# One gate chain for both directions of the mLSTM, the backward rows in reversed time

## The reference

```
gates = (g[0], log_sigmoid(g[1]), g[2], log_sigmoid(g[3]))   # input, forget; forward, backward
b = cumsum(fc);  m_t = max(b + m, running max of (b_t - b_s + i_s));  m_new = m_t of the last step
h_b, st_b = mlstm_scan(_flip(q), _flip(k), _flip(v), _flip(logi_b), _flip(logf_b), init_b, ...)
h = h_f + _flip(h_b)
```

## Time and profile before

| | |
|---|---|
| median of three runs | 2566.61 us |
| the profiled execution's own time | 2568.26 us |
| its span | 2566.5 us |
| TensorE busy, mean granted clock | 2237.9 us (87%), 0.922 |
| VectorE, ScalarE busy | 1160.2 us (45%), 887.2 us (35%) |
| HBM read | 672.15 MB, 262 GB/s over the span |
| x mixers (by the trace) | from about 1812 and 2186 us |

### The profile page before, as it was taken

The page is one execution under the profiler, slowest core; times in us unless marked ns, Lnnn a source line. Parts: engine busy times, 40 slices in busy tenths (PEclk is TensorE's granted clock), DMA queues, the critical chain, the costliest instruction groups (busy, mean ns, idle before and its releaser), DMA issues. The chain is left out here.

```text
span 2566.5 us, 45132 instructions
## 1 busy us (share of the span) xinstructions
PE 2237.9 (87%) x19490; PEld 1800.9 (70%) x19490; DVE 1160.2 (45%) x2084; ACT 887.2 (35%) x1478; POOL 58.3 (2%) x78
## 2 busy tenths in 40 slices
PE   6998788887786899879999999787897999888998
PEld 6967465554553887766766766464777998767997
DVE  5355345323331653543333322532677554766554
ACT  4444232233210542332222211232544443534442
POOL 0000000000000000000000000000000000000000
PEclk9999888989897999989999999888888999988999
DMA  7594998999999656758999999977632555323551
GB/s 237 161 337 161 365 347 337 355 377 391 405 373 363 229 185 225 283 190 327 393 395 393 390 384 376 349 284 297 206 99 84 185 177 171 132 68 115 181 173 41
DMA packets 254367, 676.24 MB, mean 263 GB/s; under 512 B 12624, under 2 KB 65872, under 8 KB 254160
## 3 DMA queue, kind: packets, MB, share of 16 engines
q1 hardware_dynamic: 238832, 614.75, 64.7%
q0 software_dynamic: 15328, 58.50, 6.7%
HBM read 672.15 MB, written 1.05 MB: 262 GB/s over the span
## 5 line engine op out<-in xcount | busy, mean ns | idle before, releaser
L444 PE MATMUL bank<-xx,high 128*128 128x256 f32 (+1 forms) x3296 | 640.9, 296 | 41.1 <-DVE xx L583 26.3
L444 PEld LDWEIGHTS bank<-xx,high 128*128 128x128 f32 (+1 forms) x3296 | 530.6, 197 | 100.1 <-issue 71.5
L444 PE MATMUL bank<-xx,low 128*128 128x256 f32 (+1 forms) x1648 | 479.1, 291 | 0.0
L444 PEld LDWEIGHTS bank<-xx,low 128*128 128x128 f32 (+1 forms) x1648 | 325.3, 197 | 1.6
L393 DVE TENSOR_TENSOR low<-lane,high 128x1024 fp32r<-128x1024 f32 (+1 forms) x112 | 130.7, 1170 | 366.8 <-ACT high L382 366.8
L382 ACT ACTIVATE high<-lane 128x1024 fp32r<-128x1024 f32 (+1 forms) x112 | 113.0, 1012 | 336.1 <-PE bank L444 336.1
L444 PE MATMUL bank<-hx,high 128*128 128x256 f32 x1056 | 201.3, 292 | 0.0
L444 PEld LDWEIGHTS bank<-hx,high 128*128 128x128 f32 x1056 | 167.4, 194 | 18.1 <-issue 16.3
L444 PE MATMUL bank<-hx,low 128*128 128x256 f32 x528 | 150.9, 286 | 0.0
L1335 ACT ACTIVATE hs<-bank 64x256 f32<-64x256 f32 x64 | 24.2, 377 | 317.6 <-PE bank L1322 317.5
L1342 DVE TENSOR_TENSOR hs<-hs,bank 64x256 f32<-64x256 f32 x64 | 27.1, 423 | 224.4 <-ACT hs L1335 224.4
(11 more groups left out here) (539 smaller groups left out, 4126.7 us busy)
## 6 DMA issues: line engine op xcount, KB each, us to landing
ring__13<-in_expert_w_gu SPq DMA_DIRECT2D x52, 1024.0 KB, 11.1
ring__12<-in_expert_w_gu SPq DMA_DIRECT2D x51, 1024.0 KB, 11.2
ring__14<-in_expert_w_gu SPq DMA_DIRECT2D x51, 1024.0 KB, 11.4
ring__56<-in_expert_w_gu SPq DMA_DIRECT2D x26, 1024.0 KB, 10.7
ring__12<-in_expert_w_down SPq DMA_DIRECT2D x26, 1024.0 KB, 9.8
ring__154<-in_expert_w_gu SPq DMA_DIRECT2D x26, 1024.0 KB, 12.7
ring__55<-in_expert_w_gu SPq DMA_DIRECT2D x25, 1024.0 KB, 10.8
ring__14<-in_expert_w_down SPq DMA_DIRECT2D x25, 1024.0 KB, 9.7
```

The lines of the kernel that those rows point to most:

```text
L444: done = pe.matmul(out, a.bitcast(F32R), b.bitcast(F32R), start=it["start"] and k == 0 and q == 0 and not halves, stop=stop)
```

## The change

The 16 gate rows are put on 8 partitions of two buffers: rows 0 to 3 forward, rows 4 to 7 backward, the backward ones in reversed time. A new table of zeros and ones, `gsel`, and a second matmul that reads `graw` from right to left do that. One chain then serves both directions over steps s = 0, 1 (for the backward direction chunk 1 - a); it has 19 operations and 20 turns. The copy to nw and the difference that follows it now share a turn. Behind `in_done` ScalarE writes m_t and U once more from right to left (the two lines added in `act`), and the gate columns of d = 1 come from those; `decay_pe` reads nw from right to left for d = 1. In `ln_at` the 32 becomes 20. Besides, ones_r and zeros shrink from 128 columns to one, which is broadcast where it is read. The diff, without its unchanged lines:

```diff
@@ -45,7 +45,7 @@
-          ("eps", 1), ("jota", NX), ("flip", 1), ("odd", 1), ("pick", 16)):
+          ("eps", 1), ("jota", NX), ("flip", 1), ("odd", 1), ("pick", 16), ("gsel", 32)):
@@ -158,11 +158,11 @@
-row, ones_r, pick = space(ctx, "row", NROW), space(ctx, "ones_r", P), space(ctx, "pick", 16)
+row, ones_r, pick = space(ctx, "row", NROW), space(ctx, "ones_r", 1), space(ctx, "pick", 16)
...
-zeros = space(ctx, "zeros", P)
+zeros = space(ctx, "zeros", 1)
@@ -174,7 +174,7 @@
-    return row[q:q + 2, o + a:o + (wd if n is None else a + n)].bitcast(F32R), ones_r[q:q + 2, :].bitcast(F32R)
+    return row[q:q + 2, o + a:o + (wd if n is None else a + n)].bitcast(F32R), ones_r[q:q + 2, :].bitcast(F32R).to_broadcast([2, P])
@@ -415,7 +415,7 @@
-                pe.matmul(z, zeros[:, 0:z.shape[0]].bitcast(F32R), some.bitcast(F32R), start=True, stop=False)
+                pe.matmul(z, zeros.bitcast(F32R).to_broadcast([P, z.shape[0]]), some.bitcast(F32R), start=True, stop=False)
@@ -817,9 +817,9 @@
-        act.activation(ones_r.bitcast(F32R), ones, ACT.Copy)
+        act.activation(ones_r.bitcast(F32R), ones[:, 0:1], ACT.Copy)
...
-        act.activation(zeros.bitcast(F32R), V("mask_z"), ACT.Copy).then_inc(*zero_a.up("zeros"))
+        act.activation(zeros.bitcast(F32R), V("zero"), ACT.Copy).then_inc(*zero_a.up("zeros"))
@@ -2115,7 +2115,7 @@
-    in_done = [(ev_a, proj.out(at_[where[-1]], last_o, 1)), (gate_v, K(0, 18)), (gate_v, K(1, 18)), (lastm_v, K(1))]
+    in_done = [(ev_a, proj.out(at_[where[-1]], last_o, 1)), (gate_v, K(18)), (lastm_v, K())]
@@ -2125,7 +2125,7 @@
-    ln_at = (ends["gate"] + 3 + -(-(32 + conv_ops) // rate)) // 2 * 2 + 1
+    ln_at = (ends["gate"] + 3 + -(-(20 + conv_ops) // rate)) // 2 * 2 + 1
@@ -2153,11 +2153,10 @@
     def gate_rows_pe(pe):
...
-        for j in range(4):
-            q0 = 64 * (j // 2)
-            bank = take(pe, bk, K("row", j))
-            pe.matmul(bank[q0:q0 + 4, 0:T], ident[0:16, 4 * j:4 * j + 4], graw[0:16, :], start=True, stop=True,
-                      tile_position=(0, q0)).then_inc(*gr_p.up(K(j)))
+        for j in range(2):
+            bank, sel = take(pe, bk, K("row", j)), V("gsel", 16 * j, 16)[0:16]
+            pe.matmul(bank[0:8, 0:T], sel[:, 0:8], graw[0:16, :], start=True, stop=False)
+            pe.matmul(bank[0:8, 0:T], sel[:, 8:16], graw[0:16, ::-1], start=False, stop=True).then_inc(*gr_p.up(K(j)))
@@ -2182,11 +2181,11 @@
     def decay_pe(pe, i, hp):
...
-        q0 = 64 * d
+        s, time = turned(d, a)
...
-            n = pe.matmul(bank[:, 256 * j:256 * j + 256], picked(q0, 4, 2 * hp + j),
-                          nw[q0:q0 + 36, a].rearrange("p c t -> p (c t)").bitcast(F32R), start=True, stop=True)
+            n = pe.matmul(bank[:, 256 * j:256 * j + 256], picked(0, 8, 4 * d + 2 * hp + j),
+                          nw[0:40, s, :, time].bitcast(F32R), start=True, stop=True)
@@ -2261,12 +2260,13 @@
         for d in range(2):
-            q0 = 64 * d
...
-            for i, r_ in enumerate((rM, rU)):
+            if d:
+                pe.wait_ge(*gate_a.at(K("turned")))
+            for i, r_ in enumerate((g_in, g_f) if d else (rM, rU)):
...
-                    n = pe.matmul(bank[:, 8 * i + 4 * a:8 * i + 4 * a + 4], r_[q0:q0 + 4, a * P:(a + 1) * P],
-                                  ident[q0:q0 + 4, q0:q0 + 4], start=True, stop=True)
+                    n = pe.matmul(bank[:, 8 * i + 4 * a:8 * i + 4 * a + 4], r_[0:8, a * P:(a + 1) * P],
+                                  ident[0:8, 4 * d:4 * d + 4], start=True, stop=True)
@@ -2308,21 +2308,17 @@
     def gate_rows_act(act):
-        for j in range(4):
-            q0 = 64 * (j // 2)
+        for j in range(2):
...
-            act.activation((g_f if j % 2 else g_in)[q0:q0 + 4, :], bk[K("row", j)][q0:q0 + 4, 0:T], ACT.Copy).then_inc(*gr_a.up(K(j)))
+            act.activation((g_f if j else g_in)[0:8, :], bk[K("row", j)][0:8, 0:T], ACT.Copy).then_inc(*gr_a.up(K(j)))
...
-        for d in range(2):
-            B = rB[64 * d:64 * d + 4, :]
-            act.wait_ge(*gate_v.at(K(d, 1)))
-            act.activation(B, B, ACT.Exp, scale=-1.0).then_inc(*gate_a.up(K(d, "exp")))
-        for d in range(2):
-            B = rB[64 * d:64 * d + 4, :]
-            act.wait_ge(*gate_a.at(K(d, "exp")))
-            act.activation(B, B, ACT.Ln, bias=ones[64 * d:64 * d + 4, 0:1]).then_inc(*gate_a.up(K(d, "ln")))
+        B = rB[0:8, :]
+        act.wait_ge(*gate_v.at(K(1)))
+        act.activation(B, B, ACT.Exp, scale=-1.0).then_inc(*gate_a.up(K("exp")))
+        act.wait_ge(*gate_a.at(K("exp")))
+        act.activation(B, B, ACT.Ln, bias=ones[0:8, 0:1]).then_inc(*gate_a.up(K("ln")))
@@ -2394,6 +2390,8 @@
         events_wait(act, in_done)
+        act.activation(g_in[0:8, :], rM[0:8, ::-1], ACT.Copy)
+        act.activation(g_f[0:8, :], rU[0:8, ::-1], ACT.Copy).then_inc(*gate_a.up(K("turned")))
@@ -2450,70 +2448,61 @@
-    def gate_chains(dve):
...
-        gens = [gate_chain(dve, d) for d in range(2)]
-        for _ in range(16):
-            for g in gens:
-                next(g, None)
-                yield
-        for g in gens:
-            run(g)
...
-    def gate_chain(dve, d):
-        q0 = 64 * d
+    def gate_chain(dve):
...
-            inst.then_inc(*gate_v.up(K(d, n[0])))
+            inst.then_inc(*gate_v.up(K(n[0])))
...
-            dve.wait_ge(*gate_v.at(K(d, n[0])))
+            dve.wait_ge(*gate_v.at(K(n[0])))
...
-        fi, ii = g_f[q0:q0 + 4, :], g_in[q0:q0 + 4, :]
-        B, U, MT = (r_[q0:q0 + 4, :] for r_ in (rB, rU, rM))
-        NH, NL, on4 = nw[q0:q0 + 4], nw[q0 + 32:q0 + 36], ones[q0:q0 + 4, 0:1]
-        dve.wait_ge(*gr_a.at(K(2 * d + 1)))
+        fi, ii = g_f[0:8, :], g_in[0:8, :]
+        B, U, MT = (r_[0:8, :] for r_ in (rB, rU, rM))
+        NH, NL, on8 = nw[0:8], nw[32:40], ones[0:8, 0:1]
+        dve.wait_ge(*gr_a.at(K(1)))
...
-        yield
-        yield
-        yield
-        dve.wait_ge(*gate_a.at(K(d, "ln")))
+        for _ in range(6):
+            yield
+        dve.wait_ge(*gate_a.at(K("ln")))
...
-            dve.wait_ge(*lastm_v.at((L, 0, d)))
-        prev = last[q0:q0 + 4, :] if v else V("zero")[q0:q0 + 4, 0:1]
-        for a in ((0, 1) if d == 0 else (1, 0)):
-            s0, s1 = a * P, (a + 1) * P
-            view = slice(s0, s1) if d == 0 else slice(s1 - 1, s0 - 1 if s0 else None, -1)
-            le = s1 - 1 if d == 0 else s0
+            dve.wait_ge(*lastm_v.at((L, 0)))
+        prev = last[0:8, :] if v else V("zero")[0:8, 0:1]
+        for s in range(2):
+            z = slice(s * P, (s + 1) * P)
...
-            step(dve.tensor_tensor_scan(B[:, view], bc(on4, [4, P]), fi[:, view], 0.0, MUL, ADD))
+            step(dve.tensor_tensor_scan(B[:, z], bc(on8, [8, P]), fi[:, z], 0.0, MUL, ADD))
...
-            step(dve.tensor_tensor(U[:, s0:s1], ii[:, s0:s1], B[:, s0:s1], SUB))
+            step(dve.tensor_tensor(U[:, z], ii[:, z], B[:, z], SUB))
...
-            step(dve.tensor_tensor_scan(MT[:, view], U[:, view], U[:, view], prev, MAX, MAX))
+            step(dve.tensor_tensor_scan(MT[:, z], U[:, z], U[:, z], prev, MAX, MAX))
...
-            step(dve.tensor_copy(NH[:, a, 0, :].bitcast(F32R), MT[:, s0:s1]))
-            yield
-            step(dve.tensor_scalar(NH[:, a, 1, :].bitcast(F32R), MT[:, s0:s1], prev, None, SUB))
+            step(dve.tensor_copy(NH[:, s, 0, :].bitcast(F32R), MT[:, z]))
+            step(dve.tensor_scalar(NH[:, s, 1, :].bitcast(F32R), MT[:, z], prev, None, SUB))
+            yield
...
-            step(dve.tensor_tensor(NL[:, a, 0, :].bitcast(F32R), MT[:, s0:s1], NH[:, a, 0, :], SUB))
-            step(dve.scalar_tensor_tensor(NL[:, a, 1, :].bitcast(F32R), MT[:, s0:s1], prev, NH[:, a, 1, :], SUB, SUB))
+            step(dve.tensor_tensor(NL[:, s, 0, :].bitcast(F32R), MT[:, z], NH[:, s, 0, :], SUB))
+            step(dve.scalar_tensor_tensor(NL[:, s, 1, :].bitcast(F32R), MT[:, z], prev, NH[:, s, 1, :], SUB, SUB))
...
-            step(dve.tensor_tensor(MT[:, s0:s1], MT[:, s0:s1], B[:, s0:s1], ADD))
-            prev = MT[:, le:le + 1]
-            if a != 1 - d:
-                yield
+            step(dve.tensor_tensor(MT[:, z], MT[:, z], B[:, z], ADD))
+            prev = MT[:, s * P + P - 1:s * P + P]
+            yield
...
-        dve.tensor_copy(last[q0:q0 + 4, :], prev).then_inc(*lastm_v.up(K(d)))
-        yield
+        dve.tensor_copy(last[0:8, :], prev).then_inc(*lastm_v.up(K()))
+        yield
...
+    def turned(d, a):
...
+        s = 1 - a if d else a
+        return s, slice(None, None, -1) if d else slice(None)
@@ -2706,7 +2695,7 @@
-        chains, taps = gate_chains(dve), iter(())
+        chains, taps = gate_chain(dve), iter(())
@@ -3080,6 +3069,16 @@
+def gate_selection():
...
+    s = np.zeros((P, 4, 8))
+    for which in range(2):
+        for d in range(2):
+            for h in range(4):
+                s[8 * d + 4 * which + h, 2 * which + d, 4 * d + h] = 1.0
+    return s.reshape(P, 32)
```

(16 more changed lines are left out.)

## The result

Four runs of the changed kernel took 2533.5 us in the median (2531.46 to 2542.41), four of the kernel before 2565.64: a ratio of 0.988, 95% interval 0.985 to 0.992. Forecast were 2572.8 us, slower, with a range of 2563 to 2582. The profiled execution took 2531.46 us (span 2529.7).

What follows compares the result with a forecast made beforehand. Bound taken: VectorE mid-mixer, then TensorE in the mixers of x; expert weights nearly everywhere in the MoE stages. Mixers +13.2 and MoE -7.0 give +6.2 us: 2574.4 profiled, median 2572.8, range 2563 to 2582.

Steps and rivals of the forecast that it cites:

- small parts: Reversed copies, second gcol group, reversed reads, broadcast weights and freed SBUF: each taken as 0 or hidden, reversed reads bounded at +4.5.
- The freed SBUF and the wider vec table: Memory allocation: the smaller ones_r and zeros and the larger vec were claimed to cost or gain 0.
- the MoE term of the sum: The lane's mixers inside the two MoE stages: -7.0 us in sum, bounds -9.5 and -1.5.
- Gate chain: VectorE's gate operations in each mixer: one chain replaces two costing 11.8 us, saving 5.9 us.
- rival D: The gate chain on 8 partitions costs as much as two chains, giving 2584 us; chance 0.03.
- The wait before the sum: TensorE in the mixers of x: idles some 7.4 us before the channel sum, where it stood 1.90.
- lost cover: Mixers of x: items 18 and 19 and the SGU matmuls now follow the conv, 13.1 us against 9.1 gained.
- slow clock: Mixers of x: two stretches at the lower TensorE clock instead of one, +2.6 us each on average, bounds 0 and 4.
- Rival A: Mixers of x: TensorE doesn't wait before the channel sum; each mixer changes by -3.0, giving 2553.6 us; chance 0.1.
- rival C: Mixers of x: no second slow stretch and a little less cover lost, giving 2567.7 us, no change; chance 0.2.
- The one of 5.23: Second MoE stage: TensorE's 5.23 us wait for the xt copy, claimed to shrink by 3.1, to near 2 to 3.
- Rival B: The MoE stages' gains vanish in the expert weights, the bound before and after, giving 2579.8 us; chance 0.2.

Runs made afterwards that it cites:

- e1: The changed kernel with 832 unused bytes per partition ahead of the weight buffers, so they start where they did before: 2565.14 us, ratio to before 1.0001.
- e3: The changed kernel with 64 unused bytes ahead of the weight buffers: 2565.31 us, ratio to before 0.9998.
- e2: The kernel before with only ones_r and zeros cut to one broadcast column and 128 unused bytes, weight buffers starting as in the changed kernel: 2527.81 us.
- e8: The changed kernel with 256 unused bytes ahead of the weight buffers: 2533.1 us.
- e4: The changed kernel with the first channel sum of the mixers of x back at item 19, the lane's staying at 17: 2519.79 us.
- e11: The changed kernel with the first channel sum back at item 19 in the mixers of x and in the lane: 2519.95 us.
- e12: The changed kernel with the first channel sum of the mixers of x at item 21: 2522.61 us.
- e5: The changed kernel with 32 unused bytes ahead of the weight buffers: 2567.0 us.
- e6: The changed kernel with 128 unused bytes ahead of the weight buffers: 2562.2 us.
- e7: The changed kernel with 224 unused bytes ahead of the weight buffers: 2565.0 us.

## Why the prediction was wrong, step by step

**The failed step** is a sentence of the small parts: "The freed SBUF and the wider vec table: 0." I looked at what these tensors cost where they are read and written, and not at what stands behind them in memory. Their place was worth 31.7 us with the changed operations (after against e1 and e3) and 38.7 with the old ones (before against e2), where the operations come to a few us either way. None of my rivals had it; the range could not hold it. The view that spoke was in the profile of before: a DMA share of 1.0 beside 393 GB/s says that the rate per engine, and not a wait, is the bound of those stretches, so what changes a packet's time had to be priced.

**With the place held, the operations cost little or nothing, and where the forecast comes near that is in part luck.** At the old address, the one that I forecast for, they are e1 against before: -1.3 us (interval -4 to +5), where I said +6.2. At the new address they are after against e2: +5.7 us by the medians, about 8 by their ratios to before (0.988 and 0.985), whose intervals overlap. The two kernels did not run side by side, but every execution of after and e8 (2531.3 to 2542.4) is above every one of e2 (2527.1 to 2531.2). So the sign held there, and the size can't be told to better than some us. At the old address the MoE term of the sum was mis-sized as well: the two stages gain 13.7 us where I said 7.0 (below), and the mixers lose 10.3 over the nine profiles (147.7 + 145.5 against 141.4 + 141.5), where I said 13.2. The parts:

**Gate chain.** The timeline of VectorE, L0 after, has the operations of the earlier trace rows, once and on 8 partitions:

```profile
1786.17 0.41 DVE L2470 SCALAR_TENSOR_TENSOR g_f<-g_f,gB 8x256 f32<-8x256 f32 x1
1786.68 0.41 DVE L2478 TENSOR_TENSOR_SCAN gB<-vec,g_f 8x128 f32<-8x128 f32 x1
...
1793.92 0.14 DVE L2499 COPY last_m<-gM 8x1 f32<-8x1 f32 x1
```

0.41 us for the 256 columns and 0.41 for the scan, as on 4 partitions; rival D is out. The chain takes 7.9 us with two lows of 1.15 in it, so 5.6 of its own; 11.8 before. Forecast 5.9 saved, found 6.2.

**The wait before the sum.** TensorE's timeline in L0 and, behind the dots, in L1:

```profile
1826.80 2.05 PE L2166 MATMUL bank<-tm,vec 128*128 128x256 f32 x4 [7.55 <-DVE tm L2557]
...
1839.73 0.69 PE L2177 MATMUL bank<-wst,tm 128*64 128x128 f32 x2
...
1843.43 2.08 PE L2166 MATMUL bank<-tm,vec 128*128 128x256 f32 x4
...
2210.07 2.04 PE L2166 MATMUL bank<-tm,vec 128*128 128x256 f32 x4 [6.35 <-DVE tm L2557]
...
2223.79 0.43 PE L2177 MATMUL bank<-wst,tm 128*64 128x128 f32 x2
...
2224.51 1.97 PE L2166 MATMUL bank<-tm,vec 128*128 128x256 f32 x4
```

Forecast was 7.4 us of idling with the conv's last add as its releaser; it is 7.55 and 6.35, L2557. Counted from the mixer's first projection, the sum comes 8.7 us earlier in L0 (68.5 against 77.2) and 8.4 in L1; forecast 9.1. What lies behind it grew by 17.0 us in L0 and 12.6 in L1. Forecast were 13.1 of lost cover and 2.6 of slow clock, 15.7 in each. Rival A (no wait) is out.

**The clock** is what makes the two mixers of after differ. Busy time by stretch, columns as above, around the first sum, over the SGU matmuls and behind them, L0 and then L1:

```profile
1826.80:1829.00 2.20, 2.20 (x5) 1.82 (x6) 2.20 (x5) 0.00 (x0) 0.00 (x0) 0.50 0.00 0
1835.80:1843.40 7.60, 7.60 (x33) 3.71 (x32) 1.83 (x3) 1.06 (x1) 0.00 (x0) 0.71 0.42 138
1843.43:1849.00 5.57, 5.57 (x14) 4.44 (x14) 2.87 (x3) 2.19 (x3) 0.00 (x0) 0.50 0.00 0
2210.07:2212.00 1.93, 1.93 (x5) 1.57 (x6) 0.99 (x1) 0.00 (x0) 0.00 (x0) 0.50 0.00 1
2218.75:2224.50 5.75, 5.75 (x33) 3.01 (x32) 1.65 (x2) 1.06 (x1) 0.00 (x0) 1.00 0.34 112
2224.50:2228.00 3.50, 3.50 (x10) 2.75 (x10) 1.39 (x2) 1.46 (x2) 0.00 (x0) 0.52 0.35 120
```

The first slow stretch, behind the idling, is in both (0.50). The second begins within the SGU matmuls of L0 (0.71, with matmul pairs of 0.69 us beside 0.43) and lasts to about 1849; in L1 the SGU matmuls run at full clock, and the slow stretch begins with the sum behind them and is over at 2228. From the SGU matmuls' start to the second sum that is 7.6 us against 5.8, and from there to the next bias matmul (L446, among the matmuls of items 20 and 21) 7.9 against 6.9: 2.8 us by the clock alone. My 2.6 for each mixer was too little for L0 (17.0 - 13.1 = 3.9) and too much for L1 (12.6 - 13.1 = -0.5). Before the change it was L1 that lost more to the clock, as the prediction has it.

That L0 grew by 8.3 is no fixed price either. In e3, the same operations at a bad place, no slow stretch falls on the SGU matmuls or on items 20 and 21 behind them (1.00 from 1877.6 to 1884.0 too):

```profile
1870.30:1877.60 7.30, 7.30 (x40) 4.02 (x38) 3.27 (x4) 1.10 (x2) 0.00 (x0) 1.00 0.26 85
```

and L0 takes 144.8 us, 3.4 more than before, where after takes 149.7. So where the slow stretches fall moves L0 by up to 5 us from one execution to the next. In e3's L0 that is rival C's condition, and its 2567.7 us is near what e1 and e3 take (2565.1 and 2565.3), but by luck: it presumed a loss of 8.1 in the mixers and a gain of 7.0 in the MoE stages.

**MoE stages.** With the place held (after and e8 against e2) the first stage is 4.2 us shorter and the second 3.4; forecast 3.9 and 3.1. For the second this stands: five profiles at the good place with the shorter chain (after, e4, e8, e11, e12) have 665.3 to 666.2 us, e2 669.6. For the first it doesn't: the same five have 573.5 to 581.4, mean 578.2, against the one 580.0 of e2, so the gain can't be told from the scatter, and the agreement is luck. At a bad place (e1, e3, e5, e6, e7 against the one profile of before) the gains are 8.9 and 4.8: there the stream is the tighter bound, and I can't say which of the lane's changes it gains from. That is about the gap between +5.7 and -1.3 us above. Single waits, TensorE's timeline of after:

```profile
455.27 1.04 PE L1280 MATMUL bank<-vec,dg_t 128*128 128x128 f32 x8
...
1614.25 0.59 PE L2158 MATMUL bank<-tm,vec 16*8 16x256 f32 x2 [1.02 <-ACT kt L2092]
1614.68 0.59 PE L2159 MATMUL bank<-tm,vec 16*8 16x256 f32 x2
1615.74 0.59 PE L2158 MATMUL bank<-tm,vec 16*8 16x256 f32 x2 [0.46 <-ACT g_in L2313]
1616.17 0.59 PE L2159 MATMUL bank<-tm,vec 16*8 16x256 f32 x2
...
1638.06 1.11 PE L1280 MATMUL bank<-vec,dg_t 128*128 128x128 f32 x4 [4.07 <-DVE xt L1249]
```

The gate rows take 2.5 us, 4.2 before; forecast was 2.1 of saving, it is 1.7. The wait of 2.85 us behind the taps is gone; forecast was that 2.3 of it go. The one of 5.23 is 4.07, not 2 to 3: part of what the shorter chain gave back was taken by something else, which I did not follow. Rival B (the gains vanish in the weights) is out for the second stage, and at a bad place for both.

**The small parts** that I set at zero without the place: the reversed copies (0.42 and 0.40 us, L2393 and L2394, ahead of kn) cause no wait of TensorE in L0 of after, and reversed reads cost nothing, shown next.

## What to carry over

Before a tensor's size is changed, or one added or removed, work out where everything allocated behind it lands. Where a DMA share of 1 shows that transfers are the bound, put the destination buffers on a multiple of 256 bytes on purpose, by a gap if need be, and compare GB/s at equal DMA share. An experiment on any other change should hold these addresses still, else it measures two things. And a due place of one instruction on an engine that keeps its order is part of the change: when the work that it waits for gets shorter, moving it earlier by the same rule can cost more than the shortening gives.

## What the runs showed of the hardware

A start 32 bytes off a multiple of 256, for the weight buffers and all that lies behind them, costs the saturated stream of this kernel 5% of its rate (414 to 392 GB/s), and 224 bytes off costs the same (393). The ring or the lane buffers off by themselves cost 5 and 11 GB/s. Per packet the software queue's bear most of it (152 to 175 ns in e3, the hardware queue's 152 to 156).

A moving operand (the one that streams through the array) that is read backwards costs TensorE nothing that shows. The decay matmuls of L0 after, third group forward and fourth reversed, both at full clock:

```profile
1878.88 0.72 PE L2187 MATMUL bank<-nw,pick 40*128 40x256 f32 x4
1883.31 0.73 PE L2187 MATMUL bank<-nw,pick 40*128 40x256 f32 x4
```
